# Projection order and hand-placed side steps around a state-space scan and an indexed attention, in a three-block transformer kernel

## The reference

```python
h = x @ w_in
g_ssd, g_att, z, xbc, dt_raw, q, c_kv, q_idx, k_idx, w_idx = split_cols(h, IN_SPLITS)
# SSD branch
xbc = silu(causal_dwconv(xbc, conv_w, conv_b))            # 2048 columns: x (1024), B (512), C (512)
dt = softplus(dt_raw + dt_bias)                           # 16 heads
a = dt * -exp(a_log); a_cs = cumsum(a)                    # within chunks of 128 tokens
y = (C B^T * exp(segsum(a))) @ (x * dt) + exp(a_cs) * C @ state + d_skip * x
y = group_rms_norm(y * silu(z)) * norm_w
# DSA branch
score = sum_h relu(q_idx_h @ k_idx^T) * w_idx_h           # 16 index heads of 64
idx = top_k(score, 64)                                    # causal
s = q (c_kv w_uk)^T / 8 - slope * dist, only at idx; o = softmax(s) @ (c_kv w_uv)
# both
merged = sigmoid(g_ssd) * (y @ w_proj_ssd) + sigmoid(g_att) * (o @ w_proj_att)
x = layer_norm(ALPHA * x + merged @ w_out)
```

## Time and profile before

| | |
|---|---|
| median of 3 runs | 2850.61 us (2848.64 to 2856.88) |
| the profiled execution | 2848.64 us, of which the span of the trace is 2846.7 us |
| granted TensorE clock, mean over the span | 0.957 |
| TensorE busy | 2657.3 us (93%) |
| VectorE busy | 1961.7 us (69%) |
| ScalarE busy | 1529.6 us (54%) |
| the weight tiles of xbc | from 228.2 us on |
| `tiles1` and its side work | about 277 to 506 us |

### The profile page before, as it was taken

One profiled execution on the slowest core, in us unless ns is written; L12 is line 12 of the kernel. 1 busy time (PEld: TensorE's weight loads), 2 busy tenths in 40 slices (PEclk: granted clock), 3 DMA queues, 4 the chain that ended last, 5 costly groups with the idle time before them and its releaser, 6 DMA issues.

```text
span 2846.7 us, 34417 instructions
## 1 busy us (share of the span) xinstructions
PE 2657.3 (93%) x14799; PEld 2296.8 (81%) x14799; DVE 1961.7 (69%) x1950; ACT 1529.6 (54%) x1600; POOL 16.1 (1%) x30
## 2 busy tenths in 40 slices
PE   8999989997998998998886999999999999988998
PEld 7989877786997976997875888888888888866876
DVE  4557689555545665545547898989889898966854
ACT  4436445433443353443545777777777777745753
POOL 0000000000000000000000000000000000000000
PEclk9999999998998998999977999999999999998999
DMA  6545333452554534584405999999999999974432
GB/s 247 187 165 180 134 117 134 162 176 83 186 190 169 193 133 140 187 224 165 141 32 203 348 357 348 358 347 358 342 341 358 347 358 346 360 272 145 146 117 89
DMA packets 88639, 632.25 MB, mean 222 GB/s; under 512 B 9793, under 2 KB 9809, under 8 KB 13473
## 3 DMA queue, kind: packets, MB, share of 16 engines
q1 hardware_dynamic: 84496, 610.24, 58.5%
q0 software_dynamic: 3984, 19.76, 2.6%
HBM read 625.77 MB, written 4.19 MB: 221 GB/s over the span
## 4 chain that ended last, share of the span: by engine, by line
PE 82%; DVE 12%; ACT 3%; DMA 1%; issue 1%; DVEq 0%; SPq 0%; ACTq 0%
PE pw L707 14%; PE pw L708 14%; PE pw L709 14%; PE py L707 11%; PE py L708 11%; PE py L709 11%; DVE lo L689 3%; ACT hi L686 1%; PE pw L878 1%; DMA raw<-in_wts 1%; PE pw L2383 1%; DVE st L913 1%; DVE X L927 1%; DVE X L920 1%; PE pw L2320 1%
## 5 line engine op out<-in xcount | busy, mean ns | idle before, releaser
L689 DVE TENSOR_TENSOR lo<-raw,hi 128x2048 fp32r<-128x2048 f32 x414 | 942.4, 2278 | 452.4 <-ACT hi L686 451.8
L686 ACT ACTIVATE hi<-raw 128x2048 fp32r<-128x2048 f32 x414 | 786.3, 1900 | 453.6 <-PE py L709 366.0
L707 PE MATMUL pw<-XH,hi 128*128 128x256 f32 x1688 | 484.2, 287 | 14.0 <-DVE lo L689 4.9
L708 PE MATMUL pw<-XL,hi 128*128 128x256 f32 x1688 | 482.1, 286 | 0.0
L709 PE MATMUL pw<-XH,lo 128*128 128x256 f32 x1688 | 481.9, 285 | 0.0
L689 DVE TENSOR_TENSOR lo<-raw,hix 128x2048 fp32r<-128x2048 f32 x168 | 384.9, 2292 | 53.6 <-ACT hix L686 50.6
L708 PE MATMUL pw<-lo,GH 128*128 128x512 f32 x896 | 354.2, 395 | 0.0
L707 PEld LDWEIGHTS pw<-XH,hi 128*128 128x128 f32 x1688 | 328.6, 195 | 19.0 <-DVE lo L689 6.3
L686 ACT ACTIVATE hix<-raw 128x2048 fp32r<-128x2048 f32 x168 | 321.7, 1916 | 39.1 <-PE py L709 37.5
L708 PEld LDWEIGHTS pw<-XL,hi 128*128 128x128 f32 x1688 | 328.8, 195 | 1.2
L709 PEld LDWEIGHTS pw<-XH,lo 128*128 128x128 f32 x1688 | 328.5, 195 | 0.0
(11 more groups left out here) (509 smaller groups left out, 3839.0 us busy)
## 6 DMA issues: line engine op xcount, KB each, us to landing
raw<-in_wts SPq DMA_DIRECT2D x577, 1024.0 KB, 4.8
GB<-in_rows POOLq DMA_DIRECT2D x8, 1024.0 KB, 5.1
scratch_bias<-dr POOLq DMA_DIRECT2D x1, 3072.0 KB, 36.0
BI<-scratch_bias POOLq DMA_DIRECT2D x1, 2048.0 KB, 15.4
raw<-in_wts SPq DMA_DIRECT2D x3, 512.0 KB, 3.3
raw<-in_wts SPq DMA_DIRECT2D x2, 576.0 KB, 3.5
X<-in_x SPq DMA_DIRECT2D x1, 1024.0 KB, 5.5
nrow<-in_rows POOLq DMA_DIRECT2D x2, 512.0 KB, 5.0
```

What stands on the lines that cost most here:

```text
L686: L.e.activation(hi, raw, ACT.Copy).then_inc(*L.up("hi", n))
L689: L.e.tensor_tensor(lo, raw, f32(hi), ALU.subtract).then_inc(*L.up("lo", n))
L707: T_.e.matmul(o, x[0], w[0], start=first, stop=False)
L708: T_.e.matmul(o, x[0], w[1], start=False, stop=False)
```

## The change

The side work and the tile order of the stages xbc and `tiles1` are rearranged.

1. In `sequence()` and `tiles1`, the four z tiles stand ahead of qi and ki instead of behind them.
2. On TensorE, the running sums follow xbc tile 4 instead of tile 6, and the transposes of x follow tile 6 instead of tile 7. The transposes take their four banks from the ring W instead of Y. ScalarE makes ea and de after tile 5 instead of 7, and copies xs after tile 6 instead of 8. VectorE negates the sums after tile 5 instead of 6, copies xs after 6 instead of 8, and makes xd and xe after 7 instead of behind the stage.
3. The three products of the gate (skip, add, z) of token half 0 stand together in scan step 5, those of half 1 together behind the scan. ScalarE's squares of half 0 move into scan step 7.
4. The index steps start behind the turn, after tile 14 (the first q tile), on TensorE and VectorE; formerly three of the eight stood ahead of it. c_kv's transposes follow tile 10 instead of 11. VectorE's norm stands ahead of the low half of c_kv. The first three top-k rounds stand one or two tiles later, the attention's first scores after the same tile as before.
5. The sum of an index step goes to the scratch tile `tmp2` instead of to MA.

```diff
@@ sequence()
-    s += seq_tm("misc", 8, 288, 288) + seq_fm("xbc", 8, 2048, 256)
-    s += seq_fm("qi", 8, D, 256) + seq_fm("ki", 8, 128, 128) + seq_tm("z", 8, D, 512) + seq_tm("gs", 8, D, 512)
+    s += seq_tm("misc", 8, 288, 288) + seq_fm("xbc", 8, 2048, 256) + seq_tm("z", 8, D, 512)
+    s += seq_fm("qi", 8, D, 256) + seq_fm("ki", 8, 128, 128) + seq_tm("gs", 8, D, 512)
@@ pe_before
-            for _ in range(5):
+            for _ in range(3):
                 yield
...
             yield
+            yield
             T_.wait_ge("silu", 6)
...
-                    b = Y.take(T_, ("xs", tt, f0))
+                    b = W.take(T_, ("xs", tt, f0))
@@ act_before
-            for _ in range(6):
+            for _ in range(4):
@@ dve_before
             yield from dve_dt(V)
-            yield
             V.wait_ge("cum")
...
-            yield
             yield
@@ act_scan
+                if i == 7:
+                    act_squares(A, 0)
@@ dve_scan
-                if i in (5, 6):
-                    dve_passed(V, i - 5)
-                if i == 7:
-                    dve_with_passed(V, 0)
-                yield
+                if i == 5:
+                    dve_gate(V, 0)
+                yield
@@ dve_gate now holds what dve_passed and dve_with_passed did
+        def dve_gate(V, tt):
+            if tt == 0:
+                V.wait_ge("ev", ("yp", 3))
+            V.own()
             V.e.tensor_tensor(heads16(xs[:, tt, :]), heads16(xs[:, tt, :]), per_head(drow[:, 32:48]),
                               ALU.mult).then_inc(*V.up())
...
@@ dve_index
-            o = s if c == 0 else MA[:, tt, 0:n]
+            o = s if c == 0 else tmp2[0][:, 0:n]
@@ pe_side1
             yield from pe_scan(T_)
-            yield
             pe_ckv(T_)
+            yield
+            yield
+            yield
+            yield
+            pe_turn(T_, "ssdt", part(Yt), 8, [("ssd", "y")])
             pe_index(T_, 0, 0)
-            yield
             yield
             pe_index(T_, 0, 1)
             pe_index(T_, 0, 2)
             yield
-            pe_turn(T_, "ssdt", part(Yt), 8, [("ssd", "y")])
             pe_index(T_, 0, 3)
-            yield
             pe_index(T_, 1, 0)
             yield
             pe_index(T_, 1, 1)
             yield
             pe_index(T_, 1, 2)
+            yield
             pe_index(T_, 1, 3)
-            yield
-            yield
             yield from pe_dsa(T_)
```

More of the change, by code:

```diff
@@ L1541, in dve_with_passed @@
             V.own()
+            V.e.tensor_tensor(heads16(xs[:, tt, :]), heads16(xs[:, tt, :]), per_head(drow[:, 32:48]),
+                              ALU.mult).then_inc(*V.up())
+            V.own()
             V.e.tensor_tensor(Yt[:, tt, :], Yt[:, tt, :], xs[:, tt, :], ALU.add).then_inc(*V.up())
-        def dve_gate(V, tt):
             V.wait_ge("ev", ("z", 1, 1, 0))
@@ L1694, in tiles1 @@
                 x0 = x_of(0)
+                yield from pe_tm(L, "z", XP, 8, D, 512, x0)
                 yield from pe_fm(L, "qi", XP, 8, D, 256, x0)
                 yield from pe_fm(L, "ki", XP, 8, 128, 128, x0)
-                yield from pe_tm(L, "z", XP, 8, D, 512, x0)
                 yield from pe_tm(L, "gs", XP, 8, D, 512, x0)
@@ L1704, in tiles1 @@
             else:
+                yield from ev_tm(L, "z", 8, D, 512, by_act(cols_of(Z), ACT.Silu))
                 yield from ev_fm(L, "qi", D, 256, fm_both(QI))
                 yield from ev_fm(L, "ki", 128, 128, ev_ki)
-                yield from ev_tm(L, "z", 8, D, 512, by_act(cols_of(Z), ACT.Silu))
                 yield from ev_tm(L, "gs", 8, D, 512, by_act(cols_of(SG1), ACT.Sigmoid))
@@ L1716, in pe_side1 @@
             yield from pe_scan(T_)
+            pe_ckv(T_)
             yield
-            pe_ckv(T_)
+            yield
+            yield
+            yield
+            pe_turn(T_, "ssdt", part(Yt), 8, [("ssd", "y")])
             pe_index(T_, 0, 0)
-            yield
             yield
@@ L1740, in act_side1 @@
             yield
-            act_squares(A, 0)
+            act_ckv(A)
             act_squares(A, 1)
             act_ssd_norm(A)
-            act_ckv(A)
             yield
@@ L1758, in dve_side1 @@
             yield from dve_scan(V)
-            dve_gate(V, 0)
+            dve_gate(V, 1)
             yield
-            dve_with_passed(V, 1)
-            dve_gate(V, 1)
             yield
@@ L1765, in dve_side1 @@
             yield
-            dve_index(V, 0, 0)
+            yield
+            dve_ssd_norm(V)
             yield
             dve_ckv_low(V)
-            dve_ssd_norm(V)
+            yield
+            yield
+            yield
+            dve_turn(V, "ssdt", 8, SSH, SSL)
+            dve_index(V, 0, 0)
             yield
@@ L1772, in dve_side1 @@
             dve_index(V, 0, 1)
-            yield
             dve_index(V, 0, 2)
             yield
-            dve_turn(V, "ssdt", 8, SSH, SSL)
             yield
             dve_index(V, 0, 3)
+            dve_index(V, 1, 0)
             yield
-            dve_index(V, 1, 0)
+            yield
+            dve_index(V, 1, 1)
             yield
@@ L1783, in dve_side1 @@
             yield
-            dve_index(V, 1, 1)
+            dve_index(V, 1, 2)
             yield
@@ L1787, in dve_side1 @@
             yield
-            dve_index(V, 1, 2)
-            yield
             dve_index(V, 1, 3)
[L1791 to L1794, removed]
             att = ev_dsa(V)
@@ L1797, in dve_side1 @@
             yield
+            dve_largest(V, 1, 0)
             yield
```

## The result

| | before | after |
|---|---|---|
| median | 2849.09 us (2846.99 to 2856.88, 5 runs) | 2870.46 us (2865.22 to 2873.91, 5 runs) |
| the profiled execution, and its span | 2848.64, 2846.7 | 2869.92, 2867.8 |

Slower: the medians differ by 21.4 us. The ratio, which is not formed from the two medians, is 1.0067, and its 95% interval of 1.0051 to 1.0084 is 14.5 to 23.9 us. The forecast was 2874, with +24.5 us.

A forecast was written before the change was run, and what follows sets the result against it. VectorE's lateness was taken to cause TensorE's waits from 225 to 620 us. Lags of 22.6 us at the first gs tile, 23.3 at MG and 24.5 in all gave 2873.1 to 2875.1, so 2874, range 2860 to 2885.

The forecast's parts named there:

- Part 1: Running sums behind xbc tile 4: TensorE waits 12.0 us for av instead of 0.5, +11.5, and +3.3 of clock.
- The upper bounds of 3.4 us on the clock terms: Low clock behind waits: 1.5 to 3.4 us after the cum wait, 0 to 3.4 after the bank waits.
- Part 2: Transposes of x behind tile 6 in W banks: bank waits of 1.1, 0.75 and 3.65 us, +5.5, and +1.7 of clock.
- The rule on rotating banks: Skill page's advice that independent groups rotate through banks; the prediction read it as against transposes in the xbc tiles' ring.
- Part 3: Start of the scan: first cb product waits 1.3 us, masked E's wait goes, -1.7, ki behind the eighth mask +1.0.
- Part 4: Index scores behind the turn: q0 and turn 17.8 us later, then +7.7 less 2.2 of filled gap, MG 23.3 later.
- The new one adds three index steps: From the turn to MG, VectorE gets three index steps of 1.13 + 1.09 + 0.29 us and small gaps: +7.7.
- The 8.4 us wait at the second attention scores: TensorE waits about 8.4 us for the last index step's bank, replacing a 5.0 us wait, under the later MG wait.
- rival C: The 8.4 us wait at the scores isn't hidden under MG: +33 us, 2882; chance 0.15.
- The end: After MG, orders as before, about 1.5 us more clock less 0.3 of a later MG wait: sum +24.5 us.
- Rival A: The lag melts, index steps don't delay MG and old waits and clock come back: +3.8 us, 2853; chance 0.10.
- Rival B: Faster: av is there on time, cum wait under some 3 us: -11.0 us, 2839; chance 0.03.

The follow-up runs named there:

- h2: Kernel before with only the new xbc stage (running sums behind tile 4, x transposes behind tile 6 in W banks): 2872.48 us against 2850.04, ratio 1.0083.
- a4: Changed kernel with the transposes of x in the Y banks, all else changed: 2866.81 us against 2850.04 for before, ratio 1.0060.
- h1: Changed kernel with the whole xbc stage put back as before, the rest still changed: 2859.25 us against 2850.04 for before, ratio 1.0033.
- h3: Changed kernel, running sums behind tile 6, x transposes right behind in Y banks, xd and xe behind tile 8: 2852.85 us against 2848.71 for before, ratio 1.0011.
- b1: Changed kernel with the first three index steps moved ahead of the turn: 2872.04 us against 2848.71 for before, ratio 1.0070.
- b3: Changed kernel with TensorE's and VectorE's side order from scan step 11 on put back as before: 2872.40 us against 2849.98 for before, ratio 1.0072.
- a3: Changed kernel with running sums behind tile 6 again, x transposes right behind, still in W banks: 2860.60 us against 2850.04 for before, ratio 1.0036.
- o1: Kernel before with VectorE's copies of two q tiles and two uv halves given to ScalarE: 2849.66 us against 2848.71, ratio 0.9999.
- c2: Kernel before with q and uv copies on ScalarE and index steps, ScalarE's turn copies and last index product moved: 2845.44 us against 2849.98, ratio 0.9981.
- p1_pool: Kernel before with the low halves of uk, uv and four ps tiles made by GpSimd instead of VectorE: 2851.71 us against 2848.71, ratio 1.0007.

## Why the prediction was right, and where it was not

**Part 1, right.** The cum wait is 12.02 us where 12.0 stood in the forecast, and av had not moved. The clock behind it cost less, 2.5 us instead of 3.3: tiles 5 and 6 took 13.7 us where two such tiles take 11.8, and 0.6 lie in the small matmuls. (The upper bounds of 3.4 us on the clock terms come from no row; 2.5 and 1.5 were measured.)

**Part 2, right in mechanism; its total is right with some luck.** The ring waits are 1.09, 0.24 and 3.57, together 4.9 instead of 5.5, and the clock 1.5 instead of 1.7 (the two tiles behind took 13.27). But the sixteen transposes, broken up by the waits, took 2.3 us without them, against 1.7 before (269.92 to 271.59), and the sum had no term for that. So 7.1 came where 7.2 stood. The rule on rotating banks that the prediction names doesn't itself speak against this ring: in W too, each group takes another bank, and what cost time was the wait for the bank's reader. h2 and a4 show the waits to belong to the xbc stage and the W banks. What I did not see is the other side of this edit: h1 shows that with z in front the Y banks would be late by 5.8 us. a4 and h3, whose transposes are in Y too but one tile earlier, have no such wait.

**Part 3, right.** The first cb product waits 1.33 (1.3), the eighth mask makes a wait of 0.91 (1.0), and the wait at the states is gone. gs0 is 22.4 later where 22.6 was forecast, 0.5 of it from before the change's first step.

**Part 4, the size right by luck, the attribution half right.** From the turn to MG the new order is 5.8 us longer (22.8 less 17.0) where 7.7 less 2.2, 5.5, was forecast. VectorE's work there did grow by about what was said, from 61.2 to 68.6 us. But the table of these stretches says that the new order costs 7.3 at a like clock, and that the clock behind the turn, full after and low before, gave 1.5 back, which the forecast did not have. And the sentence "The new one adds three index steps" names only a part: with these three back in front (b1) only 2.8 of the 7.3 go, and VectorE's gaps grow in their place; with all index steps, the norm and the top-k rounds back (b3) the stretch is as long as before (turn and MG both 20.4 later). Which of the later moves makes the other 4.5 was not tried one by one. The 8.4 us wait at the second attention scores came as 8.2, under MG's lateness, so rival C's added 8.4 us did not appear.

**The end, too large by 3.4 us.** The sum took the lag at MG as lasting and added clock. The clock behind MG did cost more than before, but 0.9 us instead of 1.5: ps tile 1 took 5.49 against 4.60. Up to the turn of o1 that leaves 1.1 us too much. Then the unchanged stages gave 2.3 us back between the turn of o1 and the end: 2.9 in the first two windows shown above, less 0.6 elsewhere. The prediction had put them at the same length as before. b3, in which they took 3.4 us more than before, shows that the difference has no fixed sign.

Rival A (the lag melts) is excluded by the kernel after itself, whose turn is 17.0 and whose MG 22.8 us late; h2 shows besides that the new xbc stage alone makes the whole loss and that the old side order doesn't give it back either (MG 20.1 us late). Rival B needed a cum wait under 3 us, and it was 12.0.

## What to carry to other kernels

When a step of an in-order engine is moved ahead, look up when its operand is written, not in which step of the program it is used: here the operand stood 12 us away, and the move cost this wait and 2.5 us of clock; with it and the ring waits in, nothing later gave the time back (h2). A ring of banks is shared by all who take from it, so each newcomer inherits the wait for its oldest holder's reader, as in a3, where putting cum back took away 11.5 us of wait and made one of 5.0 us. Where two engines hold each other up, taking work from one gave nothing (o1); moving the steps on which the other waits as well gave 5 us (c2).

## What the runs showed of the hardware

GpSimd subtracts a 128 x 2048 tile in 4.6 us, where VectorE takes 2.28, and some of VectorE's operations stand still meanwhile. In p1_pool, GpSimd's timeline and then VectorE's:

```profile
402.61 4.63 POOL L690 TENSOR_TENSOR lo<-raw,hi 128x2048 fp32r<-128x2048 f32 x1 [179.10 <-ACT hi L687]
...
416.64 4.50 POOL L690 TENSOR_TENSOR lo<-raw,hi 128x2048 fp32r<-128x2048 f32 x1 [1.92 <-ACT hi L687]
```

```profile
405.54 1.98 DVE L1640 TENSOR_TENSOR sc<-sc,kd 128x256 f32<-128x256 f32 x1
...
417.20 0.29 DVE L1647 MAX8 m<-sc 128x8 f32<-128x128 f32 x1
...
417.92 3.31 DVE L1653 TENSOR_SCALAR sc<-sc 128x128 f32<-128x128 f32 x1
```

The two long ones (405.54 and 417.92) take 0.42 and 0.23 us in the kernel before; they end at 407.52 and 421.23, just behind GpSimd's ends at 407.24 and 421.14, while the MAX8 between was not lengthened. The Trainium skill, "SBUF — State Buffer", SBUF: two separate sides, has one port pair of the two engines held as an exclusive lock for a whole instruction, by whichever starts first: a GpSimd operation, or a VectorE operation in a two-port mode or with two SBUF inputs. The TENSOR_TENSOR, with two inputs in SBUF, and the MAX8, with one, agree; in which mode the TENSOR_SCALAR ran the trace doesn't say. VectorE is rid of 2.28 us six times, 13.7 us, and its instructions that ended with one of GpSimd's are 14.0 us longer than before in all. Whether that alone used the gain up was not separated from the later low halves. The trace is also that of the slowest of ten executions (2857.62 us, median 2851.71): its turn is 4.3 us late (389.77 against 385.51) before GpSimd has started on its first tile.

The clock behind a wait is not set by the wait's length alone, nor by the length and the instructions just ahead of it. Behind the turn's wait of 1.95 us the granted clock over 5.5 us was 0.70 before and 1.00 after. Before, sixteen small index matmuls and a wait of 3.0 us lay just ahead of q0; after the change full-size matmuls ran without a wait from 377.2 to 399.6 us, up to the turn. That looks like the reason, but two other kernels speak against it: h2 has the index matmuls and a wait of 2.7 us ahead of q0, as before, and a4 has the order of the kernel after. Behind the same wait of 1.95 us, h2 and then a4:

```profile
407.86:413.36 5.50, 5.50 (x43) 5.30 (x44) 5.43 (x9) 0.68 (x2) 0.00 (x0) 1.00 0.05 19
395.38:400.88 5.50, 5.50 (x31) 5.30 (x32) 5.39 (x10) 0.68 (x2) 0.00 (x0) 0.70 0.08 31
```

And in p1, behind the 3.06 us wait for the index score at q0, with the same instructions ahead as before, the clock fell, where it was 1.00 before (376.54 to 382.04):

```profile
378.40:383.90 5.50, 5.50 (x26) 5.50 (x26) 5.36 (x10) 0.00 (x0) 0.00 (x0) 0.50 0.00 0
```

What decides it stays open. For a forecast it makes the clock behind a wait of 2 or 3 us a term between nothing and, here, 2.4 us (q0 took 8.25 us in p1 and 5.86 before).
